# ConvFFN up products of 11 of 22 channel tiles formed from seven half products, with sums on VectorE

## The reference, cut to what matters

```python
def conv_ffn(xn, prev, wup, cw, cb, wdown):
    t = xn.shape[1]
    hid = xn @ wup
    hp = jnp.concatenate([prev.astype(hid.dtype), hid], axis=1)
    c = cb
    for j in range(CONV_W):
        c = c + hp[:, j:j + t] * cw[j]
    gate, val = jnp.split(c, 2, axis=-1)
    out = (jax.nn.gelu(gate, approximate=True) * val) @ wdown
    return out, hp[:, t:]
```

## Time and profile before

| | us |
|---|---|
| median of 3 runs | 4412.34 |
| the three runs | 4408.06, 4412.34, 4420.19 |
| the profiled execution | 4419.84 |
| its span, first to last instruction | 4418.1 |
| mean granted TensorE clock, share of full | 0.962 |
| TensorE busy in the span | 4016.9 (91%) |
| VectorE busy | 1564.0 (35%) |
| ScalarE busy | 849.7 (19%) |

### The profile page before, as it was taken

One profiled execution on the slowest core, in us unless ns is written; L12 is line 12 of the kernel. 1 busy time (PEld: TensorE's weight loads), 2 busy tenths in 40 slices (PEclk: granted clock), 3 DMA queues, 4 the chain that ended last, 5 costly groups with the idle time before them and its releaser, 6 DMA issues. The chain is left out here.

```text
span 4418.1 us, 76225 instructions
## 1 busy us (share of the span) xinstructions
PE 4016.9 (91%) x34104; PEld 2621.2 (59%) x34104; DVE 1564.0 (35%) x2469; ACT 849.7 (19%) x2034; POOL 136.0 (3%) x137
## 2 busy tenths in 40 slices
PE   5999678778789999999997999999747999999998
PEld 2566466666656666665564666666535666666556
DVE  5100366666424333330112344435513433333001
ACT  1000233433212111110111222222212111111000
POOL 0000000000001000000000000000001000000001
PEclk8999899999999999999998999999869999999999
DMA  1121211110020111112221111111082011111223
GB/s 63 49 78 69 73 32 33 38 32 25 12 98 25 35 40 35 39 39 92 105 105 52 35 47 46 36 47 46 12 313 90 30 40 36 39 40 41 106 97 127
DMA packets 85442, 264.69 MB, mean 60 GB/s; under 512 B 37000, under 2 KB 43528, under 8 KB 76552
## 3 DMA queue, kind: packets, MB, share of 16 engines
q1 hardware_dynamic: 85128, 259.96, 17.1%
HBM read 224.34 MB, written 35.58 MB: 59 GB/s over the span
## 5 line engine op out<-in xcount | busy, mean ns | idle before, releaser
L280 PE MATMUL ps<-sb_h,sb_w 128*128 128x384 f32 (+1 forms) x4224 | 1289.8, 468 | 1.8 <-issue 1.8
L280 PEld LDWEIGHTS ps<-sb_h,sb_w 128*128 128x128 f32 x4224 | 801.7, 190 | 485.2 <-issue 2.8
L312 PE MATMUL ps<-sb_big,sb_w 128*128 128x384 f32 (+1 forms) x2112 | 646.6, 468 | 1.2 <-ACT sb_tmp L399 1.2
L1555 PE MATMUL ps<-sb_h,sb_w 128*128 128x384 f32 (+1 forms) x1728 | 574.1, 478 | 16.3 <-DMA sb_tmp<-c_amask 13.7
L312 PEld LDWEIGHTS ps<-sb_big,sb_w 128*128 128x128 f32 x2112 | 400.2, 190 | 241.6 <-ACT sb_tmp L399 2.2
L1555 PEld LDWEIGHTS ps<-sb_h,sb_w 128*128 128x128 f32 x1728 | 315.1, 191 | 197.1 <-issue 27.7
L487 DVE COPY sb_tmp<-sb_tmp 128x2 f32<-128x2 f32 x88 | 14.9, 169 | 761.1 <-ACT sb_tmp L399 761.1
L621 PE MATMUL ps<-sb_big,sb_w 128*128 128x384 f32 (+1 forms) x768 | 234.5, 468 | 0.0
L396 ACT ACTIVATE sb_tmp<-ps 128x384 f32<-128x384 f32 x176 | 86.4, 491 | 731.2 <-PE ps L280 731.2
L418 DVE TENSOR_TENSOR sb_tmp<-sb_tmp 128x384 f32<-128x384 f32 (+1 forms) x63 | 34.7, 551 | 526.8 <-ACT sb_tmp L344 525.0
L621 PEld LDWEIGHTS ps<-sb_big,sb_w 128*128 128x128 f32 x768 | 145.8, 190 | 88.5 <-issue 0.5
(11 more groups left out here) (258 smaller groups left out, 4004.1 us busy)
## 6 DMA issues: line engine op xcount, KB each, us to landing
sb_w<-wdown SPq DMA_DIRECT2D x46, 1408.0 KB, 6.0
sb_w<-wup SPq DMA_DIRECT2D x88, 512.0 KB, 3.5
sb_w<-wqkv SPq DMA_DIRECT2D x36, 512.0 KB, 3.6
sb_big<-kT SPq DMA_DIRECT2D x8, 2304.0 KB, 13.8
sb_big<-vc SPq DMA_DIRECT2D x8, 2304.0 KB, 15.2
rkv_scratch<-sb_w SPq DMA_DIRECT2D x24, 544.0 KB, 2.7
sb_w<-wrkv SPq DMA_DIRECT2D x24, 512.0 KB, 3.5
sb_x<-xT SPq DMA_DIRECT2D x2, 4352.0 KB, 18.1
```

The lines of the kernel that those rows point to most:

```text
L280: mm = pe.matmul(m.ps[:, 3 * q + b, 0:n], wt[f % 2][q][:, k, :], m.H[:, k, t0:t0 + n], start=(k == 0), stop=(k == KT - 1))
L312: mm = pe.matmul(m.ps[:, u % 6, 0:n], wdt[u % 2][:, f, :], hid[:, f, t0:t0 + n], start=(f == 0), stop=(f == FT - 1))
L1555: mm = pe.matmul(m.ps[:, ring(s, p), 0:w], wt[t][:, k, :], m.H[:, k, t0:t0 + w], start=(k == 0), stop=(k == KT - 1))
```

## The change

In both layers, tiles 2 to 12 (`SEVEN`) form their up product by Strassen's scheme in Winograd's form. A tile is seen as a product of 2 by 2 blocks: `A[q][r]` is gate or value weights (q) by the first or last four input slices (r); `B[r][c]` is those slices by the first or last 544 tokens (c). In place of eight block products there are seven, P1 to P7, each 2 token pieces (272 tokens) by 4 slices = 8 matmuls, 56 in a tile.

The added sums: `token_sums`, once a layer, forms T1 to T4 (each 128 by 2176) from `m.H` into the space of later tiles of `hid`. `weight_sums` and `last_weight_sum`, once for each tile, form S2, S3, A10 + A11 (in place) and S4 (in two parts). The results: ScalarE copies P1 into U2 and, after P2 has been accumulated on P1 in PSUM, the gate's first half (C11) into `hp`. VectorE forms U2 = P1 + P6, U3 = U2 + P7, the value's second half C22 = U3 + P5, its first half C21 = U3 - P4, and the gate's second half C12 = U2 + (P5 + P3), where P3 is accumulated on P5. `late_half` writes a second half in three instructions (272, 208 and 8 by 8 tokens). All eight banks are used, in pairs: three pairs rotate, P1 with P2, P6 with P4, and P7; the fourth is P5 with P3.

VectorE's convolution and multiply of tile f - 1 are split up and placed between the sums of tile f. The first up product of tile 2 waits for the whole of tile 1 to be copied, and tile 13, which is again of the old kind, waits for the last sum of tile 12 (C12). SyncE reloads both weight blocks only after P3 of the tile two before.

The diff, cut to its core (the parts left out move lines of ScalarE and of the convolution into functions of their own, with no change to what they issue):

```diff
 
+    SEVEN = range(2, 13)
+    NAMES = ("P1", "P6", "P7", "P5", "P2", "P4", "P3")
+    TAKES = ("U2", "U3", "C22", "C21", "C12")
+    HALF, PIECE = T // 2, T // 4
     ups = [(f, q, b) for f in range(2) for q in range(2) for b in range(2)]
     ups += [(f, q, 2) for f in range(2) for q in range(2)]
-    ups += [(f, q, b) for f in range(2, FT) for q in range(2) for b in range(NBLK)]
-    at = {u: n + 1 for n, u in enumerate(ups)}
+    events, pads = list(ups), list(ups)
+    for f in range(2, FT):
+        plain = [(f, q, b) for q in range(2) for b in range(NBLK)]
+        events += [(f, p) for p in NAMES] if f in SEVEN else plain
+        pads += [(f, "P1"), (f, "C11")] if f in SEVEN else plain
+    at = {u: n + 1 for n, u in enumerate(events)}
+    pad = {u: n + 1 for n, u in enumerate(pads)}
+    part = {(f, c): 5 * n + j + 1 for n, f in enumerate(SEVEN) for j, c in enumerate(TAKES)}
+    HOME = {}
+    trio = (0, 1, 2)
+    for f in SEVEN:
+        HOME[f] = {"P1": trio[0], "P2": trio[0], "P6": trio[1], "P4": trio[1], "P7": trio[2], "P5": 3, "P3": 3}
+        trio = (trio[2], trio[0], trio[1])
+
+    def last_up(f, q):
+
+        return at[f, "P3"] if f in SEVEN else at[f, q, 2]
+
...
+        parted, sums_done = sem("parted"), sem("sums")
...
+        TS = [tiles(m.big, 13 * T + j * 4 * HALF, 4, HALF) for j in range(4)]
+        U2, U3 = (m.big[:, 21 * T + j * HALF:21 * T + (j + 1) * HALF].rearrange("p (e s) -> p e s", e=2) for j in range(2))
+        S2, S3 = tiles(m.lanes, 0, 4, P), tiles(m.tmp, 4 * PADW + 152, 4, P)
+        S4 = (tiles(m.w, 4 * D + T, 3, P), tiles(m.tmp, 4 * PADW + 152 + 4 * P, 1, P))
+        two = lambda ap: ap.rearrange("p (e s) -> p e s", e=2)
+        B = [[m.H[:, 4 * r:4 * r + 4, c * HALF:(c + 1) * HALF] for c in range(2)] for r in range(2)]
+        quarter = lambda f: [[wt[f % 2][q][:, 4 * r:4 * r + 4, :] for r in range(2)] for q in range(2)]
+
+        def pair_ps(f, p):
+
+            return m.ps[:, 2 * HOME[f][p]:2 * HOME[f][p] + 2, 0:PIECE]
+
...
-                        sp.wait_ge(up, at[f - 2, q, 2])
+                        sp.wait_ge(up, last_up(f - 2, q))
...
-                if f:
-                    pe.wait_ge(padded, at[f - 1, q, b])
+                if f and f - 1 in SEVEN:
+                    pe.wait_ge(padded, pad[f - 1, "C11"])
+                    pe.wait_ge(parted, part[f - 1, "C12"])
+                elif f:
+                    pe.wait_ge(padded, pad[f - 1, q, b])
...
+            def seven(f):
+                A = quarter(f)
+                first = f - 1 not in SEVEN
+                factors = {"P1": (A[0][0], B[0][0]), "P2": (A[0][1], B[1][0]), "P3": (S4, B[1][1]), "P4": (A[1][1], TS[3]),
+                           "P5": (A[1][0], TS[0]), "P6": (S2, TS[1]), "P7": (S3, TS[2])}
+                for q in range(2):
+                    pe.wait_ge(wup[f % 2][q], 16 * (f // 2 + 1))
+                if first:
+                    pe.wait_ge(padded, pad[f - 1, 1, 2])
+                for p in NAMES:
+                    if p == "P6":
+                        pe.wait_ge(sums_done, 2 * (f - SEVEN[0]) + 1)
+                    if p == "P3":
+                        pe.wait_ge(sums_done, 2 * (f - SEVEN[0]) + 2)
+                    if not first and p == "P6":
+                        pe.wait_ge(padded, pad[f - 1, "C11"])
+                    if not first and p in ("P1", "P7", "P5"):
+                        pe.wait_ge(parted, part[f - 1, {"P1": "U3", "P7": "C21", "P5": "C12"}[p]])
+                    if p == "P2":
+                        pe.wait_ge(padded, pad[f, "P1"])
+                    if p in ("P4", "P3"):
+                        pe.wait_ge(parted, part[f, {"P4": "U2", "P3": "C22"}[p]])
+                    lhs, rhs = factors[p]
+                    for e in range(2):
+                        for k in range(4):
+                            w = (lhs[k // 3][:, k % 3, :] if p == "P3" else lhs[:, k, :])
+                            mm = pe.matmul(m.ps[:, 2 * HOME[f][p] + e, 0:PIECE], w, rhs[:, k, e * PIECE:(e + 1) * PIECE],
+                                           start=(k == 0 and p not in ("P2", "P3")), stop=(k == 3), skip_group_check=True)
+                    mm.then_inc(up, 1)
...
+            for f in range(2, FT):
+                if f in SEVEN:
+                    seven(f)
+                else:
+                    for q in range(2):
+                        for b in range(NBLK):
+                            expand(f, q, b)
...
-                        pe.wait_ge(padded, len(ups))
+                        pe.wait_ge(padded, len(pads))
...
+            for f in range(2, FT):
+                if f in SEVEN:
+                    act.wait_ge(up, at[f, "P1"])
+                    if f - 1 in SEVEN:
+                        act.wait_ge(parted, part[f - 1, "C12"])
+                    act.activation(U2, pair_ps(f, "P1"), ACT.Copy).then_inc(padded, 1)
+                    if f - 1 in SEVEN:
+                        gate(f - 1)
+                    borders(f, 0)
+                    borders(f, 1)
+                    act.wait_ge(up, at[f, "P2"])
+                    act.activation(two(hp[:, 2 * (f % 2), 2:2 + HALF]), pair_ps(f, "P2"), ACT.Copy).then_inc(padded, 1)
+                    if f + 1 not in SEVEN:
+                        gate(f)
+                else:
+                    for q in range(2):
+                        for b in range(NBLK):
+                            taking(f, q, b)
...
-            for f in range(FT):
+            def token_sums():
+                T1, T2, T3, T4 = TS
+                dve.drain()
+                dve.tensor_tensor(T1, B[0][1], B[0][0], ALU.subtract)
+                dve.tensor_tensor(T3, B[1][1], B[0][1], ALU.subtract)
+                dve.drain()
+                dve.tensor_tensor(T2, B[1][1], T1, ALU.subtract)
+                dve.drain()
+                dve.tensor_tensor(T4, T2, B[1][0], ALU.subtract)
+            def weight_sums(f):
+                A = quarter(f)
+                for q in range(2):
+                    dve.wait_ge(wup[f % 2][q], 16 * (f // 2 + 1))
+                if f - 1 in SEVEN:
+                    dve.wait_ge(up, at[f - 1, "P7"])
+                dve.tensor_tensor(S3, A[0][0], A[1][0], ALU.subtract)
+                dve.tensor_tensor(A[1][0], A[1][0], A[1][1], ALU.add)
+                dve.drain()
+                dve.tensor_tensor(S2, A[1][0], A[0][0], ALU.subtract).then_inc(sums_done, 1)
+
+            def last_weight_sum(f):
+                A = quarter(f)
+                if f - 1 in SEVEN:
+                    dve.wait_ge(up, at[f - 1, "P3"])
+                dve.drain()
+                dve.tensor_tensor(S4[0], A[0][1][:, 0:3, :], S2[:, 0:3, :], ALU.subtract)
+                dve.tensor_tensor(S4[1], A[0][1][:, 3:4, :], S2[:, 3:4, :], ALU.subtract).then_inc(sums_done, 1)
+
+            def late_half(f, q, u, p, signal):
+
+                row, ps = hp[:, 2 * (f % 2) + q, :], pair_ps(f, p)
+                cut = SEQ - HALF - PIECE
+                dve.tensor_tensor(row[:, 2 + HALF:2 + HALF + PIECE], u[:, 0, :], ps[:, 0, :], ALU.add)
+                dve.tensor_tensor(row[:, 2 + HALF + PIECE:2 + SEQ], u[:, 1, 0:cut], ps[:, 1, 0:cut], ALU.add)
+                by_batch = lambda ap: ap.rearrange("p (b s) -> p b s", b=NB)
+                dve.tensor_tensor(pview(row)[:, :, 2:2 + NS], by_batch(u[:, 1, cut:PIECE]), by_batch(ps[:, 1, cut:PIECE]),
+                                  ALU.add).then_inc(signal, 1)
+
+            def convolve(f, q):
...
+                dve.wait_ge(padded, pad[f, "C11"] if f in SEVEN else pad[f, q, 2])
+                if f in SEVEN:
+                    dve.drain()
...
+            token_sums()
+            for f in range(FT):
+                delayed = f in SEVEN and f - 1 in SEVEN
+                if f in SEVEN:
+                    dve.wait_ge(up, at[f, "P6"])
+                    dve.wait_ge(padded, pad[f, "P1"])
+                    dve.tensor_tensor(U2, U2, pair_ps(f, "P6"), ALU.add).then_inc(parted, 1)
+                    if delayed:
+                        convolve(f - 1, 0)
+                    dve.wait_ge(up, at[f, "P7"])
+                    dve.drain()
+                    dve.tensor_tensor(U3, U2, pair_ps(f, "P7"), ALU.add).then_inc(parted, 1)
+                    dve.wait_ge(up, at[f, "P5"])
+                    dve.drain()
+                    late_half(f, 1, U3, "P5", parted)
+                    if f + 1 in SEVEN:
+                        weight_sums(f + 1)
+                    if delayed:
+                        convolve(f - 1, 1)
+                        gated(f - 1)
+                    dve.wait_ge(up, at[f, "P4"])
+                    dve.tensor_tensor(two(hp[:, 2 * (f % 2) + 1, 2:2 + HALF]), U3, pair_ps(f, "P4"), ALU.subtract).then_inc(parted, 1)
+                    dve.wait_ge(up, at[f, "P3"])
+                    late_half(f, 0, U2, "P3", parted)
+                    if f + 1 in SEVEN:
+                        last_weight_sum(f + 1)
```

(6 more changed lines are left out.)

73 lines of the change are left out of this document (40 added, 33 removed).

## The result

| | before | after |
|---|---|---|
| median (us) | 4415.17 (4 runs, 4408.06 to 4420.19) | 4340.68 (4 runs, 4339.59 to 4349.85) |
| ratio, 95% interval | | 0.9837 (0.9817 to 0.9857) |
| the profiled execution, its span | 4419.84, 4418.1 | 4340.66, 4338.8 |
| first up product to first down product, each layer | 647.89 | 610.62 |

A forecast was written before the change was run, and what follows sets the result against it. TensorE's matmul stream was taken to bound the kernel: 78.0 us saved over 22 tiles, less 4.3 us at the edges, steady-tile waits 0, gave 73.7 us less, 4339 us; range 4328 to 4350 us, 87 in 100.

The forecast's parts named there:

- The pace: 272-column matmul instructions in tiles 2 to 12 follow at 229.6 ns; a tile takes 25.71 us, saving 3.55 us.
- The loads: Weight loads rising from 96 to 112 a tile cost nothing under matmuls; bound at most 162 ns a load.
- VectorE's added work: Sums add 7.4 us to VectorE's 10.5 us per tile, in all 17.9 us of 25.7, below TensorE.
- The timing table: Layout of a steady tile: VectorE's sums come in time, least to spare 6.1 us at P3, cost 0.
- The edges: TensorE waits entering tile 2 (0.75 us) and at tile 13 (1.4 us): 2.15 us a layer, 4.3 us.
- The token sums: Four instructions, 9.6 us once a layer, fit into VectorE's 11.67 us of idle time, by 2 us.
- The sum: Whole kernel: 78.0 - 4.3 = 73.7 us less; 4346 us on the profiled execution's scale, 4339 us on the median's.
- (1) VectorE late: Rival: VectorE is late at one product of each steady tile, 15 to 30 us, 4354 to 4369; 6 in 100.
- (2) Pace: Rival: narrower matmuls don't hold 229.6 ns; each ns more costs 2.5 us, 240 ns gives 4364; 2 in 100.
- (3) Loads don't overlap: Rival: loads don't lie under matmuls of the same rows, costing 3.04 us a tile, 4405 us; 1 in 100.
- (4) A wait at every product: Rival: TensorE waits for VectorE seven times a tile at 0.75 us, 37 us more, 4450 us; 2 in 100.
- (5): Rival: the stream isn't shortened, as some tile still does eight products or more columns, 4412 us; 2 in 100.

The follow-up runs named there:

- e4: Changed kernel without token sums, weight sums and TensorE's waits for them, plain blocks as factors; sums of results stay: 4342.97 us.
- e1: Changed kernel with P1 computed twice in each Strassen tile, so eight products in place of seven: 4422.89 us.
- e7: Changed kernel with each product in four pieces of 136 columns in place of two of 272, doubling matmuls and weight loads: 4350.21 us.
- e8: Changed kernel with the seven-product scheme in tile 2 alone of each layer: 4402.43 us, one run.
- e9: Changed kernel with three idle reductions (7.4 us) added on VectorE ahead of U3 in each steady tile: 4354.87 us.
- e3: Changed kernel with four idle reductions (9.9 us) added on VectorE ahead of U3 in each steady tile: 4426.41 us.
- e5: Changed kernel where tile 2's first products and tile 13's groups wait only for the banks they write: 4338.69 us.
- e10: Changed kernel with four idle reductions (9.9 us) added on VectorE before U2 in each steady tile: 4379.81 us.

## Why the prediction was right, point by point

- **What bounds the stage**: right. TensorE is busy for all of the 250 us in the ten tiles, and leaving out VectorE's sums (e4) moves the stage by 0.01 us.
- **The pace**: 229.6 ns forecast, 229.2 measured; a tile 25.71 and 25.67 us; saved 3.55 and 3.59 us a tile. e1 shows that it is the eighth product, e7 and e8 that the price of a column and of a tile hold at other sizes.
- **The loads**: right in direction, by a bound that was far too high (162 ns in the earlier trace rows, under 115.8 in e7). The short stretch of six matmuls with 128 columns at the norm is no steady pace.
- **VectorE's added work**: 17.9 us of a tile forecast, 16.5 measured. The sums that the trace had in kind were right (0.72 against 0.718; 512 elements 0.69 against 0.69). From U2 to U3, with a convolution half between, it takes 5.54 us, and the table had 5.4; but busy time doesn't count the short gaps between instructions, which my spans from first start to last end had in them. Late halves of 272, 208 and 64 took 0.44 + 0.36 + 0.21 = 1.02 us against 1.16.
- **The timing table**: 6.1 us to spare at P3 forecast, 6.2 measured. What I did not work out is that this row isn't the whole cover: 7 us of VectorE work go in before TensorE waits (e9), and what bounds it is the loop of P3, P1, P6, U2, the convolution half, U3 and C22 (e3).
- **The edges**: 2.15 us a layer forecast, 2.18 by e5. The parts were not as good as their sum, for their errors of 0.15 and 0.13 us cancel, which is luck. Entry: after the 41 old instructions P1 could start at 1399.58 + 41 x 0.2694 = 1410.63; it starts at 1411.46, 0.83 later, and takes 3.74 us in place of 3.67: 0.90 against 0.75. Exit: P3 at 1690.20 + 3.67 = 1693.87, tile 13 at 1695.07, 1.20 and the same 0.07 again, 1.27 against 1.40.
- **The token sums**: 2 us to spare forecast, 1.8 measured.
- **The sum**: 4339 us forecast, 4340.68 measured; 73.7 us saved in the forecast, 74.5 measured, by the stage length and by the medians alike (a fourth run of before moved its median from 4412.34 to 4415.17). On the profiled execution's own scale I expected 4346 and it took 4340.66. The stages explain 74.5 of its 79.2 us less; the rest lies outside them, 3.8 of it before the first up product of layer 0 (1352.32 before, 1348.55 in the row above), where the code is the same. The runs of before alone are 12 us apart, so I take it for the difference between executions; no run isolates it.
- **The rivals.** (1) VectorE late: the direction is real, but it takes 7 us more of work a tile. (2) Pace: no. (3) Loads don't overlap: no, by e7. (4) A wait at every product: none in steady tiles; and the price I gave, 0.75 us a wait, is not one number: 0.42 us where it only just bites (e9), 2.9 us for a wait of 2.68 where the clock stands (e3, 28.58 - 25.67), 4.6 us where it falls (30.27 - 25.67). (5) No: seven groups run.

## What to carry to other kernels

Where one engine runs without a gap, count its stream alone, by the spacing of starts and not by durations, and price the rest by whether it comes in time. How much more a second engine can take is not its idle share: follow the loop from the product that frees its work back to the product that waits for it, and the place of an instruction in the list decides how much of it is in that loop (9.9 us a tile lengthened the two stages by 37 us before U2 and by 86 us behind it). Compare stage lengths between two events of the trace: as long as TensorE doesn't wait in steady tiles, the two layers agree to 0.01 us, while whole executions scatter by ten. Look at more than one wait of a kind before you price it: one tile of e3 says 30.27 us, another 28.58.

## What the runs showed of the hardware that I had not expected

- 128x128 float32 weight loads of 190 ns each, one for every matmul, ran under matmuls spaced 115.8 ns apart: more than one load is under way at a time (PEld busy 250.00 of 250 us in e7). How narrow a matmul must be until loads set its pace was not found; 136 columns isn't.
- The granted clock can fall after short waits in an otherwise full stream, and equal waits need not have equal effects. In e3 TensorE waits about 2.7 us once a tile; in 15 of 20 tiles the clock then falls (0.55 over 3.1 us and 0.87 over the next 2.4 in the tile shown) and the product after it takes up to 5.44 us, in five it stays at 1.00 and the product takes 3.74. In e10 two waits of 3.72 us, at the same place of either layer, were followed by 1.00 and by 0.50. Waits of 1.6 to 2.0 us once a tile left it at 1.00 in every tile (e10). So the length of a wait doesn't decide alone; what does, no run here shows.
